# First attention of a two-block kernel: turnings by half tiles, weight splits on GpSimd, a new order of steps

## The reference, cut to what matters

```python
def attention_mixer(x, w_in, sink, rpb, w_out):
    h = x @ w_in                                   # 256 x 1024 @ 1024 x 2304
    qa, ka, va, qb, kb, vb = jnp.split(h, ...)
    qa, ka = rope(qa, pos), rope(ka, pos)
    oa = windowed_gqa_sink(qa, ka, va, sink)       # 8 query heads, 2 key heads, |i - j| <= 128
    ob = neighborhood_attention(qb, kb, vb, rpb)   # 8 heads, 4 x 16 neighbourhood
    return jnp.concatenate([oa, ob], axis=-1) @ w_out
```

## Time and profile before

| | |
|---|---|
| median of 3 runs | 1734.54 us (1733.07 to 1734.54) |
| the profiled execution | 1736.41 us, span 1734.4 us |
| PE busy | 1704.4 us, 98% of the span |
| VectorE busy | 1176.2 us, 68% |
| ScalarE busy | 923.0 us, 53% |
| GpSimd busy | 295.2 us, 17% |

### The profile page before, as it was taken

One profiled execution on the slowest core, in us unless ns is written; L12 is line 12 of the kernel. 1 busy time (PEld: TensorE's weight loads), 2 busy tenths in 40 slices (PEclk: granted clock), 3 DMA queues, 4 the chain that ended last, 5 costly groups with the idle time before them and its releaser, 6 DMA issues.

```text
span 1734.4 us, 25155 instructions
## 1 busy us (share of the span) xinstructions
PE 1704.4 (98%) x9689; PEld 1460.5 (84%) x9689; DVE 1176.2 (68%) x1565; ACT 923.0 (53%) x1269; POOL 295.2 (17%) x162
## 2 busy tenths in 40 slices
PE   8999999999999999999999999999999999999999
PEld 7767888899897788878888978888888889878887
DVE  5777765778576776577666885666666667857665
ACT  4564444545584544465445666544554456664443
POOL 5002100576260040010000740000000006500000
PEclk9999999999999999999999999999999999999999
DMA  9335655555504575536554533655465555425652
GB/s 284 136 98 170 218 193 191 154 176 159 182 2 146 167 235 193 191 125 211 187 185 168 176 116 121 206 185 191 150 214 192 193 176 165 145 97 195 193 193 97
DMA packets 204268, 293.83 MB, mean 169 GB/s; under 512 B 6474, under 2 KB 169776, under 8 KB 204192
## 3 DMA queue, kind: packets, MB, share of 16 engines
q1 hardware_dynamic: 201072, 285.56, 50.4%
q0 software_dynamic: 2688, 6.47, 1.5%
q10 hardware_dynamic: 432, 0.75, 0.2%
HBM read 291.71 MB, written 1.05 MB: 169 GB/s over the span
## 4 chain that ended last, share of the span: by engine, by line
PE 89%; DVE 5%; ACT 4%; issue 1%; POOL 1%; DMA 0%; SPq 0%; ACTq 0%; DVEq 0%; POOLq 0%
PE acc L2084 30%; PE pg L2084 14%; PE pg L2158 13%; PE pg L2162 12%; PE pg L2161 6%; PE pg L2159 6%; PE acc L2582 1%; DVE w_lo L1378 1%; ACT w_hi L852 1%; PE pg L2569 1%; PE pg L2684 1%; PE pg L2204 1%; POOL w_lo L752 1%; ACT op L867 1%; DVE op L1416 1%
## 5 line engine op out<-in xcount | busy, mean ns | idle before, releaser
L1378 DVE TENSOR_TENSOR w_lo<-w_raw,w_hi 128x2048 fp32r<-128x2048 f32 x231 | 540.5, 2341 | 165.4 <-ACT w_hi L852 165.3
L852 ACT CAST w_hi<-w_raw 128x2048 fp32r<-128x2048 f32 x269 | 513.0, 1908 | 68.5 <-PE pg L2084 28.3
L2084 PE MATMUL acc<-w_hi,op 128*128 128x512 f32 x1600 | 517.6, 393 | 1.7 <-DVE op L2014 1.6
L2158 PE MATMUL pg<-op,w_hi 128*128 128x512 f32 x960 | 382.3, 398 | 7.1 <-DVE op L1408 1.9
L2162 PE MATMUL pg<-op,w_hi 128*128 128x512 f32 x960 | 379.7, 396 | 0.0
L2084 PEld LDWEIGHTS acc<-w_hi,op 128*128 128x128 f32 x1600 | 300.3, 188 | 67.2 <-issue 8.1
L2084 PE MATMUL acc<-w_lo,op 128*128 128x512 f32 x800 | 311.5, 389 | 0.0
L752 POOL TENSOR_TENSOR w_lo<-w_raw,w_hi 128x2048 fp32r<-128x2048 f32 x38 | 175.1, 4618 | 682.6 <-DVE w_lo L1378 630.3
L2161 PE MATMUL pg<-op,w_lo 128*128 128x256 f32 x960 | 267.6, 279 | 0.0
L2159 PE MATMUL pg<-op,w_lo 128*128 128x256 f32 x960 | 266.3, 277 | 0.0
L2084 PE MATMUL pg<-op,w_hi 128*128 128x256 f32 x1184 | 221.9, 286 | 3.1 <-DVE op L1416 1.2
(11 more groups left out here) (346 smaller groups left out, 1709.6 us busy)
## 6 DMA issues: line engine op xcount, KB each, us to landing
w_raw<-in_mlp_w SPq DMA_DIRECT2D x64, 1024.0 KB, 5.3
w_raw<-in_ffn_w_gate SPq DMA_DIRECT2D x44, 1024.0 KB, 5.3
w_raw<-in_ffn_w_up SPq DMA_DIRECT2D x44, 1024.0 KB, 5.3
w_raw<-in_ffn_w_down SPq DMA_DIRECT2D x44, 1024.0 KB, 4.8
w_raw<-in_ssm_w_in SPq DMA_DIRECT2D x24, 1024.0 KB, 5.4
w_raw<-in_w_in SPq DMA_DIRECT2D x20, 1024.0 KB, 5.0
w_raw<-in_attn_w_in SPq DMA_DIRECT2D x8, 1024.0 KB, 10.2
w_raw<-in_ssm_w_out SPq DMA_DIRECT2D x8, 1024.0 KB, 4.9
```

The costliest lines, as they stand in the source:

```text
L852: act.copy(w_hi[:, u % RING, :], w_raw[:, u % RING, :]).then_inc(hi_ready, 1)
L1378: dve.tensor_tensor(w_lo[:, s, :], w_raw[:, s, :], w_hi[:, s, :].bitcast(F32), ALU.subtract) \
L2084: ins = pe.matmul(psum, l, r, start=first and i == 0, stop=last and i == 2)
L2158: pe.matmul(bank, hi, joined, start=k == 0, stop=False)
```

## The change

It touches the first attention alone. `by_pool` also names units 6 to 12, so that GpSimd does their splits; GpSimd does its bias additions in two groups of four, behind the splits of units 6 and 7. The parameter blocks are turned in steps 6 and 7 and copied in steps 7 and 8. The turnings of heads 0 to 7 are done for a pair together by `prob_turn_pair`: each 128 x 128 transpose becomes two of 64 rows, one for each half of the partitions, into banks 1 and 2 of `acc`, and ScalarE's copy of a head waits for its pair and puts the two halves together. VectorE takes the scores of both heads of a pair ahead of the maxima. For heads 8 to 15 the three loops are written anew, and in the last steps the output of unit 11 is cut in two (`second_half`). The diff, with unchanged lines left out:

```diff
 def by_pool(u):
-    return U_SSM + 2 <= u < U_SSM + 17 or ...
+    return U_ATT + 6 <= u < U_ATT_OUT + 4 or U_SSM + 2 <= u < U_SSM + 17 or ...
...
-        def turn_bank(h):
-            return acc[:, 1 + h % 2, :] if h < AQ else pg[:, 0, :]
+        def turns_until(h):
+            return (h // 2 + 1) * 2 if h < AQ else h + 1
...
             pool.wait_ge(const_in, CONST_ATT)
-            for h in range(BH):
-                pool.tensor_tensor(na_bias[:, h, :, :]..., ALU.add).then_inc(bias_ready, 1)
+            for n in range(2):
+                split(U_ATT + 6 + n)
+                for h in range(4 * n, 4 * n + 4):
+                    pool.tensor_tensor(na_bias[:, h, :, :]..., ALU.add).then_inc(bias_ready, 1)
+            for u in range(U_ATT + 8, U_ATT_OUT + 4):
+                split(u)
...
             def turned_head(h):
-                act.wait_ge(pT_done, h + 1)
+                act.wait_ge(pT_done, turns_until(h))
                 if h >= 2:
                     act.wait_ge(pv_done, h - 1)
-                act.copy(probT[:, h % 2, :, :], turn_bank(h)...).then_inc(pt_ready, 1)
+                if h < AQ:
+                    act.copy(probT[:, h % 2, :, :].rearrange("p c (q r x) -> p (c q) r x", r=2, x=HD),
+                             acc[:, 1:3, (h % 2) * T:(h % 2) * T + T].rearrange("p r (b x) -> p b r x", x=HD)) \
+                        .then_inc(pt_ready, 1)
+                else:
+                    act.copy(probT[:, h % 2, :, :], pg[:, 0, :]...).then_inc(pt_ready, 1)
...
                     turned_head(a + 1)
+                    if n == 8:
+                        split(U_ATT_OUT + 2)
                     exp_head(a + 2)
...
+            for h in range(AQ, AQ + BH, 2):
+                turned_head(h)
+                turned_head(h + 1)
+                if h + 2 < AQ + BH:
+                    exp_head(h + 2)
+                    exp_head(h + 3)
+                pair_hi(h // 2)
+                if h == AQ + 2:
                     split(U_ATT_OUT + 3)
...
-                if n in (6, 7):
-                    dve.wait_ge(par_turned, 4 if n == 6 else 5)
+                if n in (7, 8):
+                    dve.wait_ge(par_turned, 4 if n == 7 else 5)
...
                     h = 2 * (n - 4)
+                    score_take(h)
+                    score_take(h + 1)
                     softmax_max(h)
                     softmax_max(h + 1)
...
+            for h in range(AQ, AQ + BH, 2):
+                more = h + 2 < AQ + BH
+                if more:
+                    score_take(h + 2)
+                    score_take(h + 3)
+                softmax_norm(h)
+                if more:
+                    softmax_max(h + 2)
+                softmax_norm(h + 1)
+                if more:
+                    softmax_max(h + 3)
+                if h > AQ:
+                    pair_lo(h // 2 - 1)
+            pair_lo((AQ + BH) // 2 - 1)
             split(U_ATT_OUT + 4)
...
+            def prob_turn_pair(h):
+                pe.wait_ge(p_ready, h + 2)
+                if h:
+                    pe.wait_ge(pt_ready, h)
+                for g in (h, h + 1):
+                    for kt in range(TT):
+                        for qt in range(TT):
+                            for r in range(2):
+                                last = g > h and kt == TT - 1 and qt == TT - 1
+                                rows, o = slice(r * HD, r * HD + HD), (g % 2) * T + (kt * TT + qt) * HD
+                                ins = pe.transpose(acc[:, 1 + r, o:o + HD],
+                                                   prob[rows, g % 4, qt, kt * P:kt * P + P], ident[rows, rows])
+                                if last:
+                                    ins.then_inc(pT_done, 1)
...
-                if n == 5:
+                if n == 6:
                     pe.wait_ge(par_in, 16 * N_PAR)
                     par_turn(0, 4)
-                if n == 6:
+                if n == 7:
                     pe.wait_ge(par_ready, 4)
                     par_turn(4, 5)
                 if n >= 5:
                     a = 2 * (n - 5)
-                    prob_turn(a)
-                    prob_turn(a + 1)
+                    prob_turn_pair(a)
                     score_pair(a + 2)
                     value_pair(a)
...
             sums(0, 1)
             score_pair(AQ + 2)
+            sums(1, 5)
+            prob_turn(AQ)
+            sums(5, 6)
+            prob_turn(AQ + 1)
+            sums(6, 7)
+            score_pair(AQ + 4)
+            value_pair(AQ)
+            sums(7, 9)
+            prob_turn(AQ + 2)
+            sums(9, 10)
+            prob_turn(AQ + 3)
+            score_pair(AQ + 6)
+            value_pair(AQ + 2)
+            sums(10, 12)
+            prob_turn(AQ + 4)
+            sums(12, 13)
+            prob_turn(AQ + 5)
+            sums(13, 14)
+            value_pair(AQ + 4)
+            sums(14, 15)
+            prob_turn(AQ + 6)
+            sums(15, 16)
+            prob_turn(AQ + 7)
+            second_half(2, 0, 2)
+            value_pair(AQ + 6)
+            second_half(2, 2, 8)
+            pe.wait_ge(ot_ready, 8)
+            output(U_ATT_OUT + 3, 14, False, True)
             warm(pg[:, 3, :], 4)
```

More of the change, by code:

```diff
@@ L173, in by_pool @@
 def by_pool(u):
-    return U_SSM + 2 <= u < U_SSM + 17 or u == U_FFN[0] + 1 or any(U_MIX[l] + 2 <= u < U_MIX_OUT[l] + OUT_UNITS - 1 for l in range(DEPTH))
+    return U_ATT + 6 <= u < U_ATT_OUT + 4 or U_SSM + 2 <= u < U_SSM + 17 or u == U_FFN[0] + 1 or any(U_MIX[l] + 2 <= u < U_MIX_OUT[l] + OUT_UNITS - 1 for l in range(DEPTH))
 N_SUMS = 4 + 3 * DEPTH
@@ L1662, in _ @@
                     dve.wait_ge(fixed_ready, 1)
-                if n in (6, 7):
-                    dve.wait_ge(par_turned, 4 if n == 6 else 5)
-                    for b in range(4) if n == 6 else (4,):
+                if n in (7, 8):
+                    dve.wait_ge(par_turned, 4 if n == 7 else 5)
+                    for b in range(4) if n == 7 else (4,):
                         dve.tensor_copy(pcol[:, b * P:b * P + ROW_BLOCKS[b]], par_block(b)[:, 0:ROW_BLOCKS[b]]) \
@@ L1678, in _ @@
                         softmax_norm(h + 1)
[L1679 to L1697, removed]
-                        .then_inc(max_ready, 1)
-                if before:
-                    link.all_but(0)
-                    normalised(g)
-                if s == 17:
-                    split(U_ATT_OUT + 2)
-                if s >= 13 and s % 2 == 1:
-                    pair_lo((s - 5) // 2)
-                if s == 17:
-                    split(U_ATT_OUT + 3)
+            for h in range(AQ, AQ + BH, 2):
[12 more added lines that the diff above has]
+            pair_lo((AQ + BH) // 2 - 1)
             split(U_ATT_OUT + 4)
@@ L2488, in sums, with second_half @@
                         ins.then_inc(unit_done, 1)
+            def second_half(n, i0, i1):
+                u = U_ATT_OUT + n
+                if i0 == 0:
+                    take(u)
+                for i in range(i0, i1):
+                    if i % 4 == 0:
+                        pe.wait_ge(ot_ready, 4 + 2 * (n - 2) + i // 4 + 1)
+                    ins = output_part(u, 8 + 2 * n, i, False, False)
+                if i1 == 8:
+                    ins.then_inc(unit_done, 1)
             sums(0, 1)
             score_pair(AQ + 2)
-            for i in range(BH // 2):
-                h = AQ + 2 * i
-                sums(1 + 4 * i, 2 + 4 * i)
-                prob_turn(h)
-                if i < 2:
-                    score_pair(h + 4)
-                sums(2 + 4 * i, 3 + 4 * i)
-                prob_turn(h + 1)
-                sums(3 + 4 * i, 4 + 4 * i)
-                if i < 3:
-                    sums(4 + 4 * i, 5 + 4 * i)
-                value_pair(h)
-            for n in range(2, OUT_UNITS):
-                pe.wait_ge(ot_ready, 4 + 2 * n - 2)
-                output(U_ATT_OUT + n, 8 + 2 * n, False, n == OUT_UNITS - 1)
+            sums(1, 5)
[26 more added lines that the diff above has]
+            output(U_ATT_OUT + 3, 14, False, True)
             warm(pg[:, 3, :], 4)
```

21 lines of the change are left out of this document (10 added, 11 removed).

## The result

The changed kernel takes 1746.07 us (median of 4 runs, 1745.69 to 1746.59), the kernel before 1734.54 (1733.07 to 1736.42): ratio 1.0066, interval 1.0049 to 1.0084, slower by 11.5 us. The forecast was 1729.3, with 1726.0 to 1733.0 as its range. The profiled execution has a span of 1744.7 us against 1734.4. All of it lies in the first attention: its output ends at 137.54 us where it ended at 127.46, 10.1 us later, and the spans differ by 10.3. The profiled execution of the kernel before lies 1.9 us above its median, so its times come out a little late beside those of the other kernels.

A forecast was written before the change was run, and what follows sets the result against it. It took TensorE (PE), busy nearly all the span, as the bound. Terms gave -4.8 us; it kept the chart's 5.85 us less, took off 0.6 for normalisations, giving -5.2: median 1734.54 to 1729.3, range 1726.0 to 1733.0.

The forecast's parts named there:

- No cost, all covered: GpSimd's splits of units 6 to 12, 4.62 us each, would be done before PE wants them; no cost.
- One cost more: VectorE's normalisations for heads 8, 14 and 15 grow beside GpSimd's splits; 0.6 us taken, bounds 0 and 3.3.
- The rival on GpSimd and normalisations: GpSimd slows VectorE's normalisations where it counts: 3.3 us in place of 0.6, so 1732.0; chance 0.12.
- The rival of the falling clock: More PE waits in the loop of heads 8 to 15 bring the low clock: +20 us, 1749; chance 0.06.
- This removes the hole: -5.9.: Later parameter turnings remove PE's 3.19 us wait for `pcol` and the low clock after it: -5.9 us.
- Half tiles, 0 with -1.9 and +3.9: Half-tile turnings of heads 0 to 7 cost about 0.97 us a pair as before: 0, bounds over four pairs.
- the 1.94 of twice the loading: Half-tile turnings priced by weight loading alone, twice the instructions being twice the loading: 1.94 us a pair.
- 0.2 to 0.35: PE's wait per pair because ScalarE's copies wait for both heads' turnings; +1.0 us over four pairs.
- The loop, +1.2 and -0.5: Loop of heads 8 to 15: PE waits 4.15 us instead of 3.0, +1.2; fewer tile shape changes, -0.5.
- First terms of -0.6: No bias additions beside VectorE's rope, so unit 6's projection begins 0.6 us earlier: -0.6 us.
- The loop's chain per pair: VectorE's chain for each pair of heads 8 to 15, from takes to next turning: 5.9 us.
- The chart's extra 1.0 us: Gain in the chart of steps beyond the terms' -4.8 us, from tile switches and starts set closer; tied to no edit.

The follow-up runs named there:

- e5: e1 with the parameter copies ahead of VectorE's split in steps 7 and 8; 1730.91 us, ratio 0.9975 to the kernel before.
- e4: The kernel before with GpSimd's splits of units 6 to 12 and its bias additions between them, nothing else; 1748.53 us, ratio 1.0074.
- e2: The changed kernel with each GpSimd split issued as eight pieces of 256 columns; 1736.57 us, ratio 1.0008 to the kernel before.
- e10: e2 with all eight bias additions early, ahead of the splits, as in the kernel before; 1732.25 us, ratio 0.9987.
- e1: The changed kernel with the splits back on VectorE and the bias additions early again; 1735.19 us, ratio 1.0000 to the kernel before.
- e3: The kernel before with the parameter turnings and copies one step later, nothing else; 1734.97 us, ratio 1.0000.
- e7: e5 with whole 128 x 128 turnings for heads 0 to 7; 1731.10 us, ratio 0.9977 to the kernel before.
- e12: e7 with heads 0 to 9 in the old order take, maximum, take, maximum; 1729.54 us, ratio 0.9973 to the kernel before.
- e6: e3 with the parameter copies ahead of VectorE's split; 1730.42 us, ratio 0.9973 to the kernel before.
- e8: e5 with the loop of heads 8 to 15 of the kernel before on PE, VectorE and ScalarE; 1732.73 us, ratio 0.9986.

## Why the prediction was wrong, point by point

- **GpSimd's splits, "No cost, all covered", plus "One cost more" at 0.6 with 0 and 3.3 as bounds: the step that failed.** It is 15.2 us (changed kernel against e5; 13.3 in e4), the bias additions placed between the splits included (4.3 us between e2 and e10, with short pieces). I looked only at whether GpSimd was in time for PE, and it was: PE never waits for `w_lo` of GpSimd. What VectorE pays was priced as a slowing in proportion to its own size, and for normalisations alone. It is a stand until GpSimd's instruction ends, so a step of 0.16 us costs up to 4.5 us, and there are several such steps a head. The low clock comes on top at three places.
- **The rows spoke, and I misread them.** The step of 1.90 us at 169.17 ends at 171.07, and GpSimd's two instructions at 163.69 end at 170.52: held for 1.35 us, then 0.55 of its own work (0.69 for the whole at 624.52, undisturbed). The split of 3.17 at 35.92 ends at 39.09, and the eight additions end at 36.94: held for 1.0 of them, then 2.2. I read both as a rate, 1.4 or 2.8 times. Comparing ends with ends tells the two apart. The 12.21 us of the eight additions hid the same thing the other way round: the first three take 1.16 each, but the sixth, begun at 30.48, takes 3.23, because VectorE's split of 29.63 to 32.66 lies over it. So "6.1" for four additions was too long; four take 4.72 in the changed kernel.
- **The rival on GpSimd and normalisations (0.12)** named the right pair of engines, but with a slowing in place of a hold, normalisations alone, and so the wrong size. The rival of the falling clock (0.06), alone on the slower side, gave 1749 with waits in the loop as its trigger. The clock fell, as a consequence of holds, in the loop and on both sides of it.
- **"This removes the hole: -5.9."** In the changed kernel it is gone, but the reason given, "copies at the start of a VectorE step", held only because the split ahead of them had gone to GpSimd. With the split on VectorE the delayed turnings bring nothing (e1, e3); with copies ahead of it, -4.3 to -4.5.
- **Half tiles, 0 with -1.9 and +3.9.** 0.55 us a pair for 0.97, near the lower bound of 0.49: rounds on the two row halves do overlap, and the 1.94 of twice the loading is not borne out. PE's wait for the pair, "0.2 to 0.35", is 0.22. Net nothing (e7).
- **The two takes ahead** got no term of their own; they cost 0.7 to 1.6 us (e12).
- **The loop, +1.2 and -0.5.** e12 and e6 are level, so near 0; behind the two takes ahead it is 1.8 better than the old one (e8).
- **First terms of -0.6** for bias additions away from rope: gone, since splits now lie over VectorE there. The 128 x 256 addition at 42.19 takes 3.93 us, under a split of 40.95 to 45.84.
- **The sum.** The loop's chain per pair, given as 5.9 us, adds up to 5.8; nothing hangs on it. The rest of the change, without GpSimd's splits and with the copies first, makes e5's 1730.9, inside the range. That is luck and no credit to the sum: e5 is another kernel, it wins 4.3 of the 5.9 expected at the hole, and nothing from the half tiles or the loop. The chart's extra 1.0 us was never tied to an edit, and no run isolates it.

Open: why a `tensor_scalar` with one tensor input (and a scalar a row) is held like one with two, while `reciprocal` and `tensor_reduce`, also with one input, are not. GpSimd instructions with one input were not tried.

## What to carry to other kernels

Before work goes to GpSimd, list each VectorE instruction of the held kinds (below) that will lie beside it, however small, and price each at the rest of GpSimd's running instruction plus its own work. Then keep GpSimd's instructions short (here 256 columns; 1024 were not short enough for a chain of two held steps), or put them where nobody waits for VectorE. When a stall is moved, follow the queue that made it: the turnings were moved past the projection, but their copies still stood behind a split, and two lines of order were worth more than seven moved operations. Test for a hold by comparing ends of instructions on both engines, not their durations.

## What was not expected of the hardware

- A `tensor_tensor` of 128 x 2 in SBUF, 0.16 us alone, took 4.45 us beside a GpSimd `tensor_tensor` of 128 x 2048, 2.29 beside pieces of 1024 and 1.13 beside bias additions of 1.19 us; each ends within 0.03 us of the end of a GpSimd instruction. GPSIMD Engine Reference, Key points, in the Trainium skill lists this pair of engines as contending when VectorE has two SBUF inputs or a two-port mode. The traces agree as far as two SBUF inputs go; no row tells in which mode the held `tensor_scalar`s ran.
- The hold has no exception in the fourteen traces (parts of the program that no edit touched are counted in each). Of the VectorE instructions that began with 0.2 us or more of a GpSimd instruction still to run, 248 had two inputs in SBUF and 50 were a `tensor_scalar` from SBUF to SBUF: all 298 ended after it. Beside the same GpSimd work, 167 `reciprocal`s took 0.16 to 0.21 us, and `tensor_reduce` and everything with an operand in PSUM ran as long as alone.
- It works both ways: a GpSimd addition of 1.2 us took 3.23 under a VectorE split (30.48 in the kernel before).
- Sixteen fp32 turnings of 64 rows by 128 columns, on alternating row halves, took 0.55 us; eight of 128 x 128, the same data, took 0.97.
